# State space decays from turned running sums and two float32r products a step

## The chip, the cores and the metric

One Trainium2 chip, one core. The metric is the device time of one launch in microseconds; the kernel before has a median of 1307.45 us over 3 runs (1307.04 to 1307.95).

## The reference

Two transformer-like blocks on a sequence of 256 rows, width 1024, float32. Only the state space branch of the first block matters here: 32 heads of 64 in 4 groups, state 128, two chunks of 128 positions.

```python
def ssd_chunked(x, dt, a, bm, cm):
    xc = (x * dt[..., None]).reshape(b, c, SSM_CHUNK, g, e, p)
    a_dt = (dt * a).reshape(b, c, SSM_CHUNK, g, e).transpose(0, 1, 3, 4, 2)
    a_cs = jnp.cumsum(a_dt, axis=-1)
    tril = jnp.tril(jnp.ones((SSM_CHUNK, SSM_CHUNK), dtype=bool))
    decay = jnp.exp(jnp.where(tril, a_cs[..., :, None] - a_cs[..., None, :], -jnp.inf))
    cb = jnp.einsum('bclgn,bcsgn->bcgls', cc, bc)
    y_diag = jnp.einsum('bcgls,bcgels,bcsgep->bclgep', cb, decay, xc)
    ...
    y_off = jnp.einsum('bclgn,bcgepn,bcgel->bclgep', cc, prev_states, jnp.exp(a_cs))
    return (y_diag + y_off).reshape(b, l, h, p)
```

For each head and chunk a 128x128 matrix of decays is needed: exp(cs[t] - cs[s]) for s <= t, where cs is the running sum of dt*a, and 0 beyond.

## The kernel before

The program is written out by hand for each engine, in a fixed order, with semaphores between them. Weights come from memory in pieces of 1 MB through four slots (`raw`). ScalarE rounds each piece to float32r (`w_hi`, line 468) and VectorE makes the rest (`w_lo`, line 478, `dve_split`); a large product is three float32r products (lines 529 to 531). A piece may be overwritten only when the piece four before it has been used.

The stage around the change follows the attention branch. TensorE computes `att1`, then `dt`, `bc0`, `bc1` and `xs0` to `xs3` (two pieces each), and turns results back between them. After `dt` VectorE makes dt (lines 1353 to 1358: bias, a minimum, then after ScalarE's exp and log a maximum) and dt*a (line 1361), then splits the two pieces of `bc1`, then convolves `bc0` (line 1394). VectorE's order there is: two merge operations after `att1` (line 1293), a reduction, the split of the second piece of `bc0`, `dve_dt`, the split of both pieces of `bc1`, the convolution of `bc0`, and so on. After `bc1` TensorE makes the running sums with positions down the partitions (`pe_cum`).

Then `pe_ssd` runs 16 steps n, each a group g of 8 heads, a chunk c and a half q of 4 heads, with products of `z0` to `z3` and `gs0` between them as filling:
- GpSimd has made `rows` = upto[s, t] * (dt*a)[s, h], 4 heads of 128 columns (`pool_ssd_rows`, recorded at line 1610), 16 operations of 128x512. The first eight wait only for dt*a, the others for the `ssd_own` that frees their buffer, in two blocks of four.
- `pe_ssd_decay` (line 1627) is one float32 product of `beyond` with these rows, which gives the segment sums in PSUM.
- ScalarE takes exp (line 1634), VectorE multiplies by the masked scores `cb` (line 1643), and TensorE applies the matrix to x*dt (`pe_ssd_own`, line 1654).
- VectorE also has, for each group, the inputs (1559), the state's inputs (1571), skip, late, gate and norm, ScalarE and TensorE the state (1527, 1535, 1549).
GpSimd's remaining work in the stage is four small roots (`pool_z`, line 1852).

The functions that the diff touches, with their callers:

Of the kernel before, what the change touches and what calls it, by code (L numbers as in the profile page):

```python
# [28 lines left out]
NEG = -1.0e30  # L29
# [80 lines left out]
class Kernel:  # L110
# [9 lines left out]
    def memory(self):  # L120
# [33 lines left out]
        half = 4 * KD * SEQ  # L154
        self.stick_l = self.put("stick_l", [P, 2, 2, 384], y_hi_at + half)
        self.stick_w = self.put("stick_w", [P, 2, 2, 384], y_lo_at + half)
        self.rows = self.put("rows", [P, 2, 4, 4, P], y_lo_at)
        self.xc = self.put("xc", [P, 2, MT, GH, SSM_HD], y_hi_at)
        self.xd = self.put("xd", [P, GH, SSM_HD], y_hi_at + 8192)
        self.state = self.put("state", [P, GW], y_hi_at + 12288)  # L160
# [5 lines left out]
        at = self.top = -(-self.top // 128) * 128  # L166
# [67 lines left out]
        self.lat_sq_rows = self.put("mla_squares", [P, MT, 4 * QK + SEQ], y_hi_at + half + 3072)  # L234
        self.rotated = self.put("mla_rotated", [P, MT, 4, 64], y_lo_at + half + 3072)
        self.lat_rows = self.put("mla_latent_rows", [P, MT, Q_RANK + KV_RANK], y_lo_at + half + 5120)
        self.top = at + 42240

    def sb(self, name, shape, dt=F32):
        tensor = self.nc.alloc_sbuf_tensor_at(name, shape, dt, offset=self.top)  # L240
# [108 lines left out]
    def semaphores(self, known):  # L349
        def new(name, unit=1):  # L350
# [30 lines left out]
            new(n) for n in ("dt_act", "dt_dve", "conv_act", "conv_dve", "conv_silu", "xs_turned", "xs_act", "xs_dve"))  # L381
        self.dt_turned = new("dt_turned")
        self.cum_made, self.cum_exp = new("cum_made"), new("cum_exp")
        (self.ssd_rows, self.ssd_cb, self.ssd_bt, self.ssd_bn, self.ssd_xc, self.ssd_xd, self.ssd_cbm, self.ssd_state, self.ssd_state_in,
         self.ssd_off, self.ssd_skip, self.ssd_late, self.ssd_kept, self.ssd_seg, self.ssd_exp, self.ssd_decay, self.ssd_own,
         self.ssd_y) = (new("ssd_" + n) for n in (
             "rows", "cb", "bt", "bn", "xc", "xd", "cbm", "state", "state_in", "off", "skip", "late", "kept", "seg", "exp", "decay",
             "own", "y"))
        self.z_tanh, self.z_read, self.z_gated, self.z_sq, self.z_mean, self.z_root, self.z_norm, self.z_turned, self.z_hi, self.z_lo = (
            new("z_" + n) for n in ("tanh", "read", "gated", "sq", "mean", "root", "norm", "turned", "hi", "lo"))  # L390
# [957 lines left out]
def dve_dt(k):  # L1348
    dve = k.nc.vector
    dt, adt, tmp = (k.dts[:, j, :, :] for j in range(3))  # L1350
    dve.wait_ge(*k.dt_turned.by())
    for m in range(MT):
        t = dve.tensor_tensor(dt[:, m, :], dt_turn_bank(k)[:, SSM_HEADS * m:SSM_HEADS * (m + 1)], k.bcast[:, 0, :], ALU.add)
    t.then_inc(*k.out_dve.at("dt"))
    dve.wait_ge(*k.out_dve.by("dt"))
    dve.tensor_scalar(tmp, dt, 30.0, None, ALU.min).then_inc(*k.dt_dve.at("min"))
    dve.wait_ge(*k.dt_act.by("ln"))
    dve.tensor_tensor(dt, dt, tmp, ALU.max).then_inc(*k.dt_dve.at("dt"))
    dve.wait_ge(*k.dt_dve.by("dt"))
    for m in range(MT):  # L1360
        dve.scalar_tensor_tensor(out=adt[:, m, :], in0=dt[:, m, :], scalar=-1.0, in1=k.bcast[:, 1, :], op0=ALU.mult,
                                 op1=ALU.mult).then_inc(*k.dt_dve.at("adt", m))


def conv_col(k, name, tap, j):
# [60 lines left out]
    dve.tensor_copy(k.y_n[:, 1, c * GW:(c + 1) * GW], k.psum_c[:, 1024 * u + 512:1024 * u + 1024]).then_inc(*k.xs_dve.at(c))  # L1426


def pe_cum(k):
    pe, adt = k.nc.tensor, k.dts[:, 1, :, :]  # L1430
    pe.wait_ge(*k.dt_dve.by("adt", 1))
    for c in range(MT):
        pe.matmul(k.psum_c[:, 32 * c:32 * c + 32], k.upto[:], adt[:, c, :], start=c == 0, stop=True, skip_group_check=True)
    pe.matmul(k.psum_c[:, 64:96], k.beyond[:], adt[:, 0, :], start=False, stop=True, skip_group_check=True).then_inc(*k.cum_made.at())


def act_cum(k):

    act = k.nc.scalar
    act.wait_ge(*k.cum_made.by())  # L1440
    act.activation(k.dts[:, 3, :, :], k.psum_c[:, 0:64].rearrange("p (c h) -> p c h", c=MT), ACT.Copy)
    act.activation(k.dts[:, 4, 0, :], k.psum_c[:, 64:96], ACT.Copy).then_inc(*k.cum_exp.at("copied"))


def act_cum_exp(k):
# [154 lines left out]
    dve.tensor_tensor(x_1, x_1, k.late[:, u, :], ALU.add).then_inc(*k.ssd_kept.at(g))  # L1600


def pool_ssd_rows(k, g):
    pool, u, adt = k.nc.gpsimd, g % 2, k.dts[:, 1, :, :]
    if g >= 2:
        pool.wait_ge(*k.ssd_own.by(g - 2, 1, 1))
    for c in range(MT):
        for q in range(2):
            heads = adt[:, c, g * GH + 4 * q:g * GH + 4 * q + 4].unsqueeze(2).to_broadcast([P, 4, P])
            pool.tensor_tensor(k.rows[:, u, 2 * c + q, :, :], k.upto[:].unsqueeze(1).to_broadcast([P, 4, P]), heads,  # L1610
                               ALU.mult).then_inc(*k.ssd_rows.at(g, c, q))
# [9 lines left out]

def pe_ssd_decay(k, n):
    (g, c, q), pe = ssd_steps()[n], k.nc.tensor
    pe.wait_ge(*k.ssd_rows.by(g, c, q))
    if n >= 2:
        pe.wait_ge(*k.ssd_exp.by(*ssd_steps()[n - 2]))
    pe.matmul(ssd_seg(k, q), k.beyond[:], k.rows[:, g % 2, 2 * c + q, :, :].rearrange("p h t -> p (h t)"), start=True,
              stop=True).then_inc(*k.ssd_seg.at(g, c, q))


def act_ssd_decay(k, n):
    (g, c, q), act = ssd_steps()[n], k.nc.scalar
    act.wait_ge(*k.ssd_seg.by(g, c, q))
    act.activation(k.rows[:, g % 2, 2 * c + q, :, :], ssd_seg(k, q).rearrange("p (h t) -> p h t", h=4),
                   ACT.Exp).then_inc(*k.ssd_exp.at(g, c, q))


def dve_ssd_decay(k, n):
    (g, c, q), dve = ssd_steps()[n], k.nc.vector
    r = k.rows[:, g % 2, 2 * c + q, :, :]  # L1640
    dve.wait_ge(*k.ssd_exp.by(g, c, q))
    dve.wait_ge(*k.ssd_cbm.by(g))
    dve.tensor_tensor(r, r, k.cb[:, g % 2, c, :].unsqueeze(1).to_broadcast([P, 4, P]), ALU.mult).then_inc(*k.ssd_decay.at(g, c, q))


def pe_ssd_own(k, n):
    (g, c, q), pe = ssd_steps()[n], k.nc.tensor
    pe.wait_ge(*k.ssd_decay.by(g, c, q))
    pe.wait_ge(*k.ssd_xc.by(g))
    if g >= 1:  # L1650
        pe.wait_ge(*k.ssd_y.by(g - 1, c))
    for h in range(4):
        at = 512 * c + (4 * q + h) * SSM_HD
        mm = pe.matmul(k.psum_c[:, at:at + SSM_HD], k.rows[:, g % 2, 2 * c + q, h, :], k.xc[:, g % 2, c, 4 * q + h, :],
                       start=q == 0 and h == 0, stop=True, skip_group_check=True)
    mm.then_inc(*k.ssd_own.at(g, c, q))

# [137 lines left out]

# [2003 lines left out]
def tensor_program(k):  # L3799
    pe, A, B = k.nc.tensor, k.psum_a, k.psum_b  # L3800
# [96 lines left out]
def scalar_program(k):  # L3897
# [27 lines left out]
    for u, dst in ((0, k.b_t), (1, k.c_t)):  # L3925
        act_conv_first(k, f"bc{u}", u, 16 + 4 * u)
        act_split(k)
        act_conv_silu(k, f"bc{u}", u, dst)
    act_cum(k)
    for c in range(4):  # L3930
        if c >= 2:
            act.wait_ge(*k.xs_turned.by(c - 2))
        act_conv_first(k, f"xs{c}", c % 2, 4 * c)
        act_split(k)
        act_conv_silu(k, f"xs{c}", c % 2, k.conv[:, c % 2, :, :])
        if c:
            act_turn_back(k, c - 1)
# [83 lines left out]
def vector_program(k):  # L4021
# [175 lines left out]
```

## Time and profile before

| | |
|---|---|
| median of 3 runs | 1307.45 us |
| the profiled execution | 1307.76 us |
| its span, first to last instruction | 1306.2 us |
| TensorE busy | 1286.4 us (98%) |
| VectorE busy | 978.1 us (75%) |
| ScalarE busy | 690.8 us (53%) |
| GpSimd busy | 173.9 us (13%) |
| HBM traffic | 211 MB, 162 GB/s |

The page gives busy time by engine; matmuls are pipelined and their ends modelled, so the distance between starts, or the chain of work that ended last, says more of TensorE than a duration. Durations on VectorE and GpSimd include any time in which the instruction was held after it started. The state space steps run from about 246 to 325 us, the dt and bc work from 159 to 186 us.

### The profile page before, as it was taken

Reading aid. Unit: us, or ns where it says so; the run is one execution under the profiler, and the core shown is the slowest. Engines: PE = TensorE matmul, PEld = TensorE weight load, DVE = VectorE, ACT = ScalarE, POOL = GpSimd, SP = SyncE. Lnnn points to the kernel's source line nnn. Section 1 sums busy time; section 2 is a strip of 40 time slices with the busy share of each in tenths; the row PEclk is TensorE's granted clock in tenths of the full one; section 3 lists DMA queues with packets and bytes.
Section 4 is the critical chain, followed back from the end, with each engine's and each line's share of the span. In section 5 each row is a group of like instructions: output and inputs, shape, how many; then the busy total and the mean of one; then the engine's idle time right before and its main releaser. Section 6 shows DMA issues by size and latency. Waiting matters only on the chain.

```text
span 1306.2 us, 19907 instructions
## 1 busy us (share of the span) xinstructions
PE 1286.4 (98%) x7874; PEld 1118.2 (86%) x7874; DVE 978.1 (75%) x1542; ACT 690.8 (53%) x1014; POOL 173.9 (13%) x241
## 2 busy tenths in 40 slices
PE   8999999999999999999999999999999989999999
PEld 8988999878998998888888877888888867888887
DVE  6457487878646757766667877798888887888888
ACT  5345556535626546633334745655554775655553
POOL 8000030022000000210001231000000160000000
PEclk9999999999999999999999999999999999999999
DMA  9532445522553536476665633266665612376662
GB/s 313 183 128 67 164 165 191 168 91 98 216 188 129 195 129 209 124 206 182 189 201 165 208 129 113 82 208 188 188 190 182 195 60 81 116 207 189 188 203 83
DMA packets 208796, 212.59 MB, mean 163 GB/s; under 512 B 7489, under 2 KB 155923, under 8 KB 208704
## 3 DMA queue, kind: packets, MB, share of 16 engines
q1 hardware_dynamic: 205632, 206.25, 49.7%
q0 software_dynamic: 2480, 4.02, 1.0%
q8 instruction: 63, 1.03, 0.3%
q10 hardware_dynamic: 592, 1.05, 0.2%
q14 instruction: 29, 0.24, 0.1%
HBM read 210.25 MB, written 1.05 MB: 162 GB/s over the span
## 4 chain that ended last, share of the span: by engine, by line
PE 69%; DVE 4%; ACT 3%; issue 2%; POOL 1%; ACTq 0%; DVEq 0%; POOLq 0%
PE psum_b L2206 9%; PE psum_a L2206 9%; PE psum_b L2209 5%; PE psum_a L2209 5%; PE psum_c L529 4%; PE psum_c L530 4%; PE psum_c L531 4%; PE psum_b L529 3%; PE psum_a L529 3%; PE psum_a L531 3%; PE psum_b L531 3%; PE psum_a L530 3%; PE psum_b L530 3%; DVE w_lo L478 1%; PE psum_c L2842 1%
## 5 line engine op out<-in xcount | busy, mean ns | idle before, releaser
L468 ACT ACTIVATE w_hi<-raw 128x2048 fp32r<-128x2048 f32 (+3 forms) x231 | 368.2, 1631 | 24.7 <-PE psum_b L531 12.9
L478 DVE TENSOR_TENSOR w_lo<-raw,w_hi 128x2048 fp32r<-128x2048 f32 (+3 forms) x154 | 342.1, 2237 | 43.8 <-ACT w_hi L468 41.2
L2206 PE MATMUL psum_b<-x,w_hi 128*128 128x512 f32 x528 | 165.6, 395 | 0.0
L2206 PE MATMUL psum_a<-x,w_hi 128*128 128x512 f32 x522 | 164.1, 396 | 0.0
L2209 PEld LDWEIGHTS psum_b<-x,w_lo 128*128 128x128 f32 x528 | 99.2, 188 | 23.2
L491 DVE TENSOR_TENSOR w_lo<-raw,w_hi 128x512 fp32r<-128x512 f32 (+1 forms) x159 | 116.5, 736 | 2.6 <-ACT w_hi L468 2.6
L2209 PEld LDWEIGHTS psum_a<-x,w_lo 128*128 128x128 f32 x522 | 98.0, 188 | 22.8
L2401 POOL CAST ffn_hidden_hi<-ffn_h 128x256 fp32r<-128x256 f32 x66 | 51.0, 773 | 485.3 <-DVE ffn_h L2388 330.3
L2357 ACT ACTIVATE ffn_pre<-ffn_both,cols 128x256 f32<-128x256 f32 x88 | 50.3, 602 | 113.0 <-DVE ffn_both L2369 113.0
L529 PE MATMUL psum_c<-w_hi,ffn_hidden_hi 128*128 128x512 f32 x264 | 103.6, 392 | 0.6 <-DVE ffn_hidden_lo L2393 0.5
L2209 PE MATMUL psum_b<-x,w_lo 128*128 128x256 f32 x528 | 103.7, 278 | 0.0
L530 PE MATMUL psum_c<-w_lo,ffn_hidden_hi 128*128 128x512 f32 x264 | 103.0, 390 | 0.0
L531 PE MATMUL psum_c<-w_hi,ffn_hidden_lo 128*128 128x512 f32 x264 | 102.8, 389 | 0.0
L2209 PE MATMUL psum_a<-x,w_lo 128*128 128x256 f32 x522 | 102.6, 278 | 0.0
L2206 PEld LDWEIGHTS psum_b<-x,w_hi 128*128 128x128 f32 x528 | 82.4, 189 | 2.1
L2206 PEld LDWEIGHTS psum_a<-x,w_hi 128*128 128x128 f32 x522 | 81.7, 189 | 2.3
L2383 DVE SCALAR_TENSOR_TENSOR ffn_pre<-ffn_both,cols,ffn_pre 128x254 f32<-128x254 f32 (+1 forms) x176 | 73.5, 478 | 0.7 <-ACT ffn_pre L2357 0.3
L2369 DVE TENSOR_REDUCE ffn_both<-psum_a 128x256 f32<-128x512 f32 x66 | 42.5, 686 | 37.7 <-PE psum_a L2209 37.7
L2369 DVE TENSOR_REDUCE ffn_both<-psum_b 128x256 f32<-128x512 f32 x66 | 42.5, 686 | 34.6 <-PE psum_b L2209 34.6
L529 PE MATMUL psum_a<-x,w_hi 128*128 128x256 f32 x224 | 64.2, 287 | 1.0 <-DVE x L699 1.0
L529 PE MATMUL psum_b<-x,w_hi 128*128 128x256 f32 x224 | 64.0, 286 | 0.0
L531 PE MATMUL psum_b<-x,w_lo 128*128 128x256 f32 x224 | 63.4, 283 | 0.0
(567 smaller groups left out, 3016.7 us busy)
## 6 DMA issues: line engine op xcount, KB each, us to landing
raw<-in_ffn_w_up_dram SPq DMA_DIRECT2D x88, 512.0 KB, 5.0
raw<-in_w_in_dram SPq DMA_DIRECT2D x39, 1024.0 KB, 5.4
raw<-in_w_gu_dram SPq DMA_DIRECT2D x44, 512.0 KB, 5.0
raw<-in_ffn_w_down_dram SPq DMA_DIRECT2D x44, 512.0 KB, 3.5
raw<-in_w_down_dram SPq DMA_DIRECT2D x22, 512.0 KB, 3.3
raw<-in_w_br_ssm_dram SPq DMA_DIRECT2D x8, 1024.0 KB, 5.0
raw<-in_w_xkv_dram SPq DMA_DIRECT2D x8, 1024.0 KB, 6.3
raw<-in_w_out_dram SPq DMA_DIRECT2D x8, 1024.0 KB, 6.4
```

The lines of the kernel that those rows point to most:

```text
L468: act.activation(k.w_hi[:, s, 0:size], k.raw[:, s, 0:size], ACT.Copy).then_inc(*k.rounded.at(*key))
L478: dve.tensor_tensor(k.w_lo[:, s, 0:size], k.raw[:, s, 0:size], k.w_hi[:, s, 0:size].bitcast(F32), ALU.subtract).then_inc(*k.split.at(*key))
L491: t = dve.tensor_tensor(k.w_lo[:, s, at], k.raw[:, s, at], k.w_hi[:, s, at].bitcast(F32), ALU.subtract)
L529: pe.matmul(out_ap, l[0], r[0], start=start, stop=False, skip_group_check=True)
L530: pe.matmul(out_ap, l[0], r[1], start=False, stop=False, skip_group_check=True)
L531: return pe.matmul(out_ap, l[1], r[0], start=False, stop=stop, skip_group_check=True)
L2206: pe.matmul(ps[:, 512 * j:512 * j + 512].rearrange("p (n t) -> p n t", n=2), hi[j], k.X_both[:, :, kt, :], start=kt == 0, stop=False, skip ...
L2209: mm = pe.matmul(ps[:, 512 * j:512 * j + SEQ], lo[j], k.X[0][:, kt, :], start=False, stop=kt == KD - 1, skip_group_check=True)
L2357: act.activation(k.pre[:, u, j, :], k.both[:, u, j, :], ACT.Identity, scale=ffn_col(k, "ffn_conv_w_2", layer, 2, j, h), bias=ffn_col(k, "f ...
L2369: dve.tensor_reduce(k.both[:, u, j, :], ps[:, 512 * j:512 * j + 512].rearrange("p (n t) -> p t n", n=2), AX, ALU.add).then_inc(*k.ffn_both ...
L2383: dve.scalar_tensor_tensor(out=k.pre[:, u, j, d:], in0=k.both[:, u, j, :SEQ - d], scalar=ffn_col(k, "ffn_conv_w_2", layer, 2 - d, j, h), i ...
L2401: pool.tensor_copy(k.hid[0][:, u, :], k.h32[:, u, :]).then_inc(*k.ffn_hi.at(tag, h))
```

## The change

The decays are made from the running sums themselves. `pe_cum` also makes the sums turned, with the 32 heads down the partitions and the 256 positions along them, from a copy of dt*a in the order half, head, group (`tmp`, two more small VectorE operations in `dve_dt`). They are kept as two float32r parts (`cum_t`; ScalarE the rounded, VectorE the rest). For each of the four (c, q) the ten rows of a product stand at partitions 32n: on one side (`sums_s`) for 4 heads the sums at s in two parts, and two rows of -1; on the other (`sums_t`) the selection of the head in two times four rows, and the sums at t in two parts. One product of these gives cs[s] - cs[t] for 4 heads; a second product ahead of it, `later_r` with the identity, adds 1e30 where s > t; ScalarE's exp has scale -1. GpSimd writes the eight selection rows (4 operations, each 8 partitions by 2048 elements, as soon as `att1` is done) and issues 16 small DMAs from SBUF to SBUF that place the sums. The buffer `rows` holds 4 steps instead of 8, and ScalarE's exp waits for the `ssd_own` four steps before.

```diff
+        self.step_ident = self.put("step_ident", [P, P], masks_at + 4 * 4 * P, F32R)
...
-        self.rows = self.put("rows", [P, 2, 4, 4, P], y_lo_at)
+        self.rows = self.put("rows", [P, 4, 4, P], y_lo_at)
+        self.sums_t = self.put("sums_t", [P, 4, SSM_GROUPS, P], y_lo_at + half, F32R)
+        self.sums_s = self.put("sums_s", [P, SSM_GROUPS, P], y_hi_at + 10240, F32R)
...
@@ dve_dt
+    for m in range(MT):
+        by_step = tmp[:, m, :].rearrange("p (q h g) -> p g q h", q=2, h=4)
+        dve.scalar_tensor_tensor(out=by_step, in0=dt[:, m, :].rearrange("p (g q h) -> p g q h", g=SSM_GROUPS, q=2), scalar=-1.0,
+                                 in1=k.bcast[:, 1, :].rearrange("p (g q h) -> p g q h", g=SSM_GROUPS, q=2), op0=ALU.mult,
+                                 op1=ALU.mult).then_inc(*k.dt_dve.at("adt_turned", m))
@@ pe_cum
-    pe.wait_ge(*k.dt_dve.by("adt", 1))
+    pe.wait_ge(*k.dt_dve.by("adt_turned", 1))
...
+    for c in range(MT):
+        pe.matmul(cum_rows(k)[:, P * c:P * c + P], k.dts[:, 2, c, :], k.upto[:], start=False, stop=True, skip_group_check=True)
...
+def act_cum_rows(k):
+    act = k.nc.scalar
+    act.activation(k.cum_t[0][0:SSM_HEADS, :], cum_rows(k), ACT.Copy).then_inc(*k.cum_act.at("hi"))
+    act.wait_ge(*k.used.by("att1", 1))
+    act.activation(k.sums_s[:, :, :], k.neg_ones[:].unsqueeze(1).to_broadcast([P, SSM_GROUPS, P]), ACT.Copy)
+    act.activation(k.step_ident[:, :], k.ident[:], ACT.Copy)
+    act.activation(k.later_r[:, :], k.strict[:], ACT.Copy, scale=-NEG).then_inc(*k.cum_act.at("ones"))
+
+def dve_cum_rows(k):
+    dve = k.nc.vector
+    dve.wait_ge(*k.cum_act.by("hi"))
+    dve.tensor_tensor(k.cum_t[1][0:SSM_HEADS, :], cum_rows(k), k.cum_t[0][0:SSM_HEADS, :].bitcast(F32),
+                      ALU.subtract).then_inc(*k.cum_dve.at("lo"))
...
-def pool_ssd_rows(k, g):
...
+def step_rows(n, at=0, count=10):
+    return slice(32 * (n % 4) + at, 32 * (n % 4) + at + count)
+
+def pool_ssd_heads(k):
+    pool = k.nc.gpsimd
+    pool.wait_ge(*k.masks.by("ident"))
+    for n in range(4):
+        r, at = step_rows(n, 0, 8), 32 * n
+        first, second = (k.ident[r, at + 4 * j:at + 4 * j + 4].unsqueeze(2).to_broadcast([8, 4, SSM_GROUPS * P]) for j in range(2))
+        pool.tensor_tensor(k.sums_t[r, :, :, :].rearrange("p h g t -> p h (g t)"), first, second, ALU.add).then_inc(*k.sums_made.at("t", n))
+
+def pool_ssd_sums(k):
+    pool = k.nc.gpsimd
+    pool.wait_ge(*k.cum_act.by("ones"))
+    pool.wait_ge(*k.cum_dve.by("lo"))
+    for n in range(4):
+        c, q = n // 2, n % 2
+        for j in range(2):
+            src = k.cum_t[j][16 * q:16 * q + 16, P * c:P * c + P]
+            pool.dma_start(k.sums_t[step_rows(n, 8 + j, 1), :, :, :].rearrange("p h g t -> p (h g) t"), src).then_inc(*k.sums_in.at("t", n, j))
+            pool.dma_start(k.sums_s[step_rows(n, 4 * j, 4), :, :], src).then_inc(*k.sums_in.at("s", n, j))
...
 def pe_ssd_decay(k, n):
     (g, c, q), pe = ssd_steps()[n], k.nc.tensor
-    pe.wait_ge(*k.ssd_rows.by(g, c, q))
+    if n == 0:
+        pe.wait_ge(*k.sums_in.by("s", 3, 1))
+        pe.wait_ge(*k.sums_made.by("t", 3))
     if n >= 2:
         pe.wait_ge(*k.ssd_exp.by(*ssd_steps()[n - 2]))
-    pe.matmul(ssd_seg(k, q), k.beyond[:], k.rows[:, g % 2, 2 * c + q, :, :].rearrange("p h t -> p (h t)"), start=True,
-              stop=True).then_inc(*k.ssd_seg.at(g, c, q))
+    r, seg = step_rows(n), ssd_seg(k, q).rearrange("p (h t) -> p h t", h=4)
+    pe.matmul(seg, k.later_r[:, :], k.step_ident[:, :].unsqueeze(1).to_broadcast([P, 4, P]), start=True, stop=False)
+    pe.matmul(seg, k.sums_s[r, g, :], k.sums_t[r, :, g, :], start=False, stop=True).then_inc(*k.ssd_seg.at(g, c, q))
 
 def act_ssd_decay(k, n):
     (g, c, q), act = ssd_steps()[n], k.nc.scalar
     act.wait_ge(*k.ssd_seg.by(g, c, q))
+    if g:
+        act.wait_ge(*k.ssd_own.by(g - 1, c, q))
...
 def gpsimd_ssd(k):
     k.nc.gpsimd.wait_ge(*k.used.by("att1", 1))
-    k.nc.gpsimd.wait_ge(*k.dt_dve.by("adt", 1))
-    pool_ssd_rows(k, 0)
-    pool_ssd_rows(k, 1)
-    pool_ssd_rows(k, 2)
-    pool_z(k, 0)
-    pool_ssd_rows(k, 3)
-    for g in (1, 2, 3):
+    pool_ssd_heads(k)
+    pool_ssd_sums(k)
+    for g in range(SSM_GROUPS):
         pool_z(k, g)
@@ tensor_program, before the first turn back
             pe.wait_ge(*k.cum_exp.by("copied"))
+            pe.wait_ge(*k.cum_dve.by("lo"))
```

`act_cum_rows` stands behind `act_cum`, `dve_cum_rows` behind the splits that follow the convolution of `bc1`.

## Rows read from the trace of the kernel before

**Rows 1.** The page: busy time of TensorE, and its clock in 40 slices.

```profile
PE 1286.4 (98%) x7874; PEld 1118.2 (86%) x7874; DVE 978.1 (75%) x1542; ACT 690.8 (53%) x1014; POOL 173.9 (13%) x241
...
PEclk9999999999999999999999999999999999999999
```

**Rows 2.** PE's waits, 160 to 340 us (total, times, longest), and line 1627's durations.

```profile
PE psum_a L529 <- DVE gated L1812: 0.5, 1, 0.5
...
L1627 PE MATMUL psum_c<-rows,beyond x32: 590/591/595, 246.6 to 317.7; 128*128 128x512 f32 x32
```

**Rows 3.** The chain that ended last, 285 to 325 us: start, us on the chain, work.

```profile
293.10 0.23 PE psum_a L531
293.33 0.86 PE psum_c L1627 x2
...
300.94 0.50 PE psum_b L1517 x4
...
306.03 1.10 PE psum_b L1527 x2
...
310.20 0.92 PE psum_b L1535 x2
...
322.98 0.84 PE psum_c L1654 x8
```

**Rows 4.** Timeline of POOL and DVE, 167 to 181 us: start, duration, instruction, times.

```profile
168.79 3.08 POOL L1610 TENSOR_TENSOR rows<-upto,dts 128x512 f32<-128x512 f32 x1
176.88 2.03 POOL L1610 TENSOR_TENSOR rows<-upto,dts 128x512 f32<-128x512 f32 x2
167.86 3.12 DVE L478 TENSOR_TENSOR w_lo<-raw,w_hi 128x2048 fp32r<-128x2048 f32 x1 [1.25 <-ACT w_hi L468]
170.90 3.12 DVE L478 TENSOR_TENSOR w_lo<-raw,w_hi 128x2048 fp32r<-128x2048 f32 x1
175.14 5.28 DVE L1394 SCALAR_TENSOR_TENSOR conv<-psum_b,cols,conv 128x255 f32<-128x255 f32 x12 [1.12 <-ACT conv L1375]
```

**Rows 5.** Timeline of DVE, 277 to 321 us.

```profile
277.33 3.12 DVE L478 TENSOR_TENSOR w_lo<-raw,w_hi 128x2048 fp32r<-128x2048 f32 x1
...
319.99 0.69 DVE L1643 TENSOR_TENSOR rows<-rows,cb 128x512 f32<-128x512 f32 x1
```

**Rows 6.** Timeline of DVE and PE, 159 to 174 us, and of ACT at 198.

```profile
159.39 1.29 DVE L1293 TENSOR_TENSOR merged<-psum_b,merged 128x512 f32<-128x512 f32 x2 [1.46 <-PE psum_b L531]
162.75 2.27 DVE L478 TENSOR_TENSOR w_lo<-raw,w_hi 128x2048 fp32r<-128x2048 f32 x1
...
166.31 0.29 DVE L1361 SCALAR_TENSOR_TENSOR dts<-dts,bcast 128x32 f32<-128x32 f32 x2
...
173.76 0.28 PE L531 MATMUL psum_b<-x,w_lo 128*128 128x256 f32 x1
173.88 0.28 PE L529 MATMUL psum_a<-x,w_hi 128*128 128x256 f32 x1
...
197.79 1.93 ACT L1375 ACTIVATE conv<-psum_b,cols 128x256 f32<-128x256 f32 x4 [5.00 <-PE psum_b L531]
```

**Rows 7.** Timeline of POOL and DVE, 27 to 32 us: GpSimd issuing DMAs beside splits.

```profile
29.48 0.61 POOL L1020 DMA_DIRECT2D bcast<-in_dt_bias_dram  x1
...
27.05 4.49 DVE L478 TENSOR_TENSOR w_lo<-raw,w_hi 128x2048 fp32r<-128x2048 f32 x2 [1.74 <-ACT w_hi L468]
```

**Rows 8.** Timeline of POOL and DVE at 762 us: a power beside a split.

```profile
762.23 2.91 POOL L2478 TENSOR_TENSOR fox_rstd<-fox_rstd,half_neg 128x16 f32<-128x16 f32 x1 [22.69 <-DVE fox_rstd L2472]
...
762.26 2.33 DVE L478 TENSOR_TENSOR w_lo<-raw,w_hi 128x2048 fp32r<-128x2048 f32 x1
```

**Rows 9.** Timeline of PE, 3 to 10 us.

```profile
3.02 0.27 PE L1045 MATMUL psum_b<-ident,stage 8*128 8x8 f32 x1 [3.02 <-POOL inv_freq L1004]
3.55 4.21 PE L804 MATMUL psum_a<-ident 128*128 128x128 f32 x18 [0.26 <-DVE cols L1053]
...
8.34 1.73 PE L804 MATMUL psum_a<-ident 128*128 128x128 f32 x14
```

More of the change, by code:

```diff
@@ L132, in memory @@
         self.res = self.sb("res", [P, MT, D])
+        masks_at = self.top
         self.ident, self.ones, self.upto, self.beyond, self.neg_from, self.neg_ones, self.strict, self.causal = (
             self.sb(name, [P, P]) for name in ("ident", "ones", "upto", "beyond", "neg_from", "neg_ones", "strict", "causal"))
+        self.step_ident = self.put("step_ident", [P, P], masks_at + 4 * 4 * P, F32R)
         self.half_neg = self.sb("half_neg", [P, 64])
@@ L156, in memory @@
         self.stick_w = self.put("stick_w", [P, 2, 2, 384], y_lo_at + half)
-        self.rows = self.put("rows", [P, 2, 4, 4, P], y_lo_at)
+        self.rows = self.put("rows", [P, 4, 4, P], y_lo_at)
+        self.sums_t = self.put("sums_t", [P, 4, SSM_GROUPS, P], y_lo_at + half, F32R)
+        self.sums_s = self.put("sums_s", [P, SSM_GROUPS, P], y_hi_at + 10240, F32R)
+        self.cum_t = [self.put(n, [P, SEQ], o, F32R) for n, o in (("cum_t_hi", y_hi_at + 15360), ("cum_t_lo", self.memory_kv_at + 2048))]
         self.xc = self.put("xc", [P, 2, MT, GH, SSM_HD], y_hi_at)
@@ L236, in memory @@
         self.lat_rows = self.put("mla_latent_rows", [P, MT, Q_RANK + KV_RANK], y_lo_at + half + 5120)
-        self.top = at + 42240
+        self.later_r = self.put("later_r", [P, P], at + 42240, F32R)
+        self.top = at + 42752
     def sb(self, name, shape, dt=F32):
@@ L383, in semaphores @@
         self.cum_made, self.cum_exp = new("cum_made"), new("cum_exp")
-        (self.ssd_rows, self.ssd_cb, self.ssd_bt, self.ssd_bn, self.ssd_xc, self.ssd_xd, self.ssd_cbm, self.ssd_state, self.ssd_state_in,
+        self.cum_act, self.cum_dve, self.sums_made, self.sums_in = new("cum_act"), new("cum_dve"), new("sums_made"), new("sums_in", 16)
+        (self.ssd_cb, self.ssd_bt, self.ssd_bn, self.ssd_xc, self.ssd_xd, self.ssd_cbm, self.ssd_state, self.ssd_state_in,
          self.ssd_off, self.ssd_skip, self.ssd_late, self.ssd_kept, self.ssd_seg, self.ssd_exp, self.ssd_decay, self.ssd_own,
          self.ssd_y) = (new("ssd_" + n) for n in (
-             "rows", "cb", "bt", "bn", "xc", "xd", "cbm", "state", "state_in", "off", "skip", "late", "kept", "seg", "exp", "decay",
+             "cb", "bt", "bn", "xc", "xd", "cbm", "state", "state_in", "off", "skip", "late", "kept", "seg", "exp", "decay",
              "own", "y"))
@@ L1426, in dve_turn_back, with cum_rows @@
     dve.tensor_copy(k.y_n[:, 1, c * GW:(c + 1) * GW], k.psum_c[:, 1024 * u + 512:1024 * u + 1024]).then_inc(*k.xs_dve.at(c))
+def cum_rows(k):
+    return k.psum_c[0:SSM_HEADS, P:P + SEQ]
 def pe_cum(k):
     pe, adt = k.nc.tensor, k.dts[:, 1, :, :]
-    pe.wait_ge(*k.dt_dve.by("adt", 1))
+    pe.wait_ge(*k.dt_dve.by("adt_turned", 1))
     for c in range(MT):
         pe.matmul(k.psum_c[:, 32 * c:32 * c + 32], k.upto[:], adt[:, c, :], start=c == 0, stop=True, skip_group_check=True)
+    for c in range(MT):
+        pe.matmul(cum_rows(k)[:, P * c:P * c + P], k.dts[:, 2, c, :], k.upto[:], start=False, stop=True, skip_group_check=True)
     pe.matmul(k.psum_c[:, 64:96], k.beyond[:], adt[:, 0, :], start=False, stop=True, skip_group_check=True).then_inc(*k.cum_made.at())
@@ L1600, in dve_ssd_late @@
     dve.tensor_tensor(x_1, x_1, k.late[:, u, :], ALU.add).then_inc(*k.ssd_kept.at(g))
-def pool_ssd_rows(k, g):
[L1604 to L1611, printed above, removed]
+def step_rows(n, at=0, count=10):
[17 more added lines that the diff above has]
+            pool.dma_start(k.sums_s[step_rows(n, 4 * j, 4), :, :], src).then_inc(*k.sums_in.at("s", n, j))
 def ssd_seg(k, q):
@@ L1633, in act_ssd_decay @@
     act.wait_ge(*k.ssd_seg.by(g, c, q))
-    act.activation(k.rows[:, g % 2, 2 * c + q, :, :], ssd_seg(k, q).rearrange("p (h t) -> p h t", h=4),
-                   ACT.Exp).then_inc(*k.ssd_exp.at(g, c, q))
+    if g:
+        act.wait_ge(*k.ssd_own.by(g - 1, c, q))
+    act.activation(k.rows[:, n % 4, :, :], ssd_seg(k, q).rearrange("p (h t) -> p h t", h=4),
+                   ACT.Exp, scale=-1.0).then_inc(*k.ssd_exp.at(g, c, q))
 def dve_ssd_decay(k, n):
     (g, c, q), dve = ssd_steps()[n], k.nc.vector
-    r = k.rows[:, g % 2, 2 * c + q, :, :]
+    r = k.rows[:, n % 4, :, :]
     dve.wait_ge(*k.ssd_exp.by(g, c, q))
@@ L1653, in pe_ssd_own @@
         at = 512 * c + (4 * q + h) * SSM_HD
-        mm = pe.matmul(k.psum_c[:, at:at + SSM_HD], k.rows[:, g % 2, 2 * c + q, h, :], k.xc[:, g % 2, c, 4 * q + h, :],
+        mm = pe.matmul(k.psum_c[:, at:at + SSM_HD], k.rows[:, n % 4, h, :], k.xc[:, g % 2, c, 4 * q + h, :],
                        start=q == 0 and h == 0, stop=True, skip_group_check=True)
@@ L3929, in scalar_program @@
     act_cum(k)
+    act_cum_rows(k)
     for c in range(4):
@@ L4058, in vector_program @@
         dve_split(k)
+    dve_cum_rows(k)
     for c in range(4):
```

## Prediction

> **What bounds the kernel now.** I read the page first, then the waits of PE between 160 and 340 us, then the chain and the timelines of this stage. TensorE is busy 98% of the span [rows 1]. In the whole stage it waits for another engine once, for 0.5 us [rows 2]. So between 160 and 340 us the time is the sum of PE's work: what PE does less comes off the end, what it waits more is added. The rest of the program hangs on PE's own signals (weight slots come free after their products), so a shift here should reach the end whole.
>
> A decay step today is one float32 product of 128x512, two records, and takes 0.86 us in the chain; a float32r product of the same width takes 0.23 us [rows 3]. There are 16 steps (32 records from 246.6 to 317.7 us) [rows 2].
>
> The second thing to read is GpSimd beside VectorE. One head-row operation of 128x512 takes 1.01 us when nothing is in its way (two in 2.03) [rows 4]. Overlapped with a split of weights, either engine stands still: a split that takes 2.2 us (two in 4.49) [rows 7] took 3.12 us while a GpSimd operation was in flight to 168.79, and the GpSimd operation behind that took 3.08 us, which is the rest of the split plus its own 1.01; the split behind it took 3.12 again although it followed at once [rows 4]. So each VectorE operation with two SBUF inputs waits for the GpSimd operation in flight, to its end, then GpSimd waits for it, in turns. The same at 277 us: again 3.12 for a split [rows 5]. The convolution operations, which read PSUM and one SBUF tile, ran beside GpSimd at their usual 5.28 us for twelve, and GpSimd at its usual 1.01 [rows 4].
>
> **The change, part by part.**
>
> (1) Decay steps. Each float32 product (0.86) becomes two float32r products, the mask product and the ten-row product. No row shows ten rows; bounds are 0.23 each (width decides) and, as the dear end, no gain at all (0.86 for both). I take 0.23, since the width is what the new products share with the row at 0.23. Gain 16 x (0.86 - 0.46) = 6.4 us.
>
> (2) GpSimd's second and third blocks of head rows, at 275 and 297 us, go. In each block the four operations hold three of VectorE's like the split at 277 us (3.12 for 2.25) [rows 5], so VectorE gets back 2.6 us a block. PE gets its own waits back: the 0.5 us [rows 2], which stood behind that late VectorE chain, and 0.18 us at each of two state products (1.10 where 0.92 is usual) [rows 3]. Gain 0.8 us. What is next late: the last decay multiplication on VectorE ends at 320.7, and its products start on PE at 322.98 [rows 3, 5], 2.3 us later. In the VectorE-bound stretch since 297 us PE gains 2.6 us (six steps and one wait) and VectorE 2.6, so that cover stays.
>
> (3) The running sums turned, in pe_cum: two float32 products with a 128-wide moving side, on the chain. The nearest row is 0.50 us for two products of 128x128 [rows 3]. Cost 0.5 us, between 0.2 (32 columns of weights) and 1.0.
>
> (4) ScalarE and VectorE get five operations between bc1 and xs0 (a copy of 32x256, one 128x512, two 128x128; a subtraction of 32x256), some 2 us. Their cover is the wait ahead of every convolution, 5.00 us on ScalarE ahead of xs0's [rows 6], 1.1 on VectorE ahead of bc0's [rows 4]. Cost 0 on the chain; without the cover under 1 us once. The new wait of ScalarE for ssd_own of the group before, and PE's for cum_dve, stand behind products that PE has done by then: 0.
>
> (5) Sixteen GpSimd DMA issues of 0.6 us [rows 7], about 10 us, after the sums, at about 203 us (bc1 from 173.9, 11.5 of products, 1.3 to the convolution, 5.3 and 4.5 for it and two splits, and the stall of part 6). Behind them on GpSimd's queue stand only the four small roots of z, in the steps; the decay products wait for them at 246.6, so there are over 25 us for landing. VectorE's splits ran at 2.25 us beside GpSimd's DMA issues at the start of the kernel [rows 7]. Cost 0.
>
> (6) pool_ssd_heads. This is the part that I price highest. Four operations over 8 partitions, but 2048 elements each along the free side: 4 x 1.01 = 4.0 us each. They wait only for att1, which ended just before VectorE's merge started at 159.39 [rows 6]; the old rows waited for dt*a, made from 166.31 on [rows 6]. So 16 us of GpSimd now lie from 159.4 over the dt chain and the splits of bc0 and bc1. In turns:
> - GpSimd 1: 159.4 to 163.4. The split of the second half of bc0, ready at 162.75, runs 163.4 to 165.6. PE wants it at 168.2 (bc1 starts at 173.88, and half a unit is 48 products of 0.12, the distance of the last two PE rows [rows 6]): no stall.
> - GpSimd 2: 165.6 to 169.6; the minimum over dt (or, if a one-input operation isn't held, the maximum after it) runs at 169.6.
> - GpSimd 3: 169.7 to 173.7; the maximum runs at 173.7.
> - GpSimd 4: 173.85 to 177.9; the four products dt*a (two old, two new, 0.1 each) end at 178.3.
> - Only then, in VectorE's order, the split for bc1: 178.3 to 180.5.
> PE has its last product of bc0 at 173.76 and starts bc1 at 173.88 [rows 6]. It now waits until 180.6: 6.7 us. If the minimum isn't held, the four turns end at the same place, since each of the four GpSimd operations still finds a VectorE operation waiting for it. The second half of bc1 is split by 182.8, when PE wants it at 186: no second stall. VectorE runs the bc0 convolution 183 to 188 and the splits of xs0 to 192.5, when PE comes to it at 192 to 195: just in time.
> The cost of (6) lies between 0 (a long GpSimd operation over 8 partitions doesn't hold VectorE: one of 2.91 us, a power, left a split beside it at 2.33 [rows 8]) and 6.7. I take 6.7, because the only streaming additions and products that the trace has beside VectorE held it to their end each time [rows 4, 5], and the power reads 16 elements and then computes.
> What the Trainium skill says of it (GPSIMD Engine Reference, Key points): GpSimd shares its SBUF interfaces with VectorE, which collide where a VectorE instruction has two SBUF inputs or a 2-port mode. The trace agrees, with 0.84 us for each held operation. Its section Performance versus the Vector engine gives 4497 ns for a float32 tensor_tensor of 2048 elements; with that the stall would be some 2 us longer than the sum has it.
>
> (7) A PE that stood for 6.7 us may come back slow. The page's clock row reads full all through [rows 1], but pitch tells: after its 3.0 us without work at the start of the kernel, PE needed 4.21 us for 18 products of 128x128 (0.23 each), and from 8.3 us on 1.73 for 14 (0.12 each) [rows 9], half rate, that is 1.2 instead of 2.4 GHz, for some 4.5 us. At half rate that loses 2.3 us. Bounds 0 and 3.4. I take 2.3, because 6.7 is more standing still than the 3.0 of that row.
> The Trainium skill (TensorE: Matmul & The Clock Gate, Part 1) has an idle engine fall to 1.2 GHz and come back under load; by that rule the 2.3 us are due, without it the sum ends at no change.
>
> **Sum.** -6.4 - 0.8 + 0.5 + 6.7 + 2.3 = +2.3 us. The profiled execution has 1307.76 us, span 1306.2 and 1.6 around it, 0.3 above the median 1307.45. The forecast is 1307.45 + 2.3 = 1309.8.
>
> **Rivals.**
> - *No hold.* The heads' operations don't hold VectorE, or only for short pieces, and (6) and (7) vanish: -6.4 - 0.8 + 0.5 = -6.7, 1300.8. For it: the power row; 8 of 128 partitions. Against: every streaming operation in rows 4 and 5. With a hold of half the length the turns end at 170 to 171, the split at 173, and PE hardly waits: also about 1301. In between (holds of 3 us) 1302 to 1306.
> - *Slower: heads dearer than 4.0 us.* If one takes 4.5 us (more than four times the short one, or both inputs broadcast), the four turns end 2 us later and PE stalls 8.7: +4.3, 1311.8. It decides from 4.1 us per operation on, where the total passes the 0.2% line.
> - *Stall, but PE returns at full clock:* +0.0, 1307.5.
> - *The change doesn't do what it says:* the ten-row or the broadcast product costs as much as the old one; then the 6.4 isn't there and even the stall-free case ends at 1307, with the stall at 1316. For it only that no row shows such a product.
>
> **How the numbers follow.** Forecast 0.40 (1308.5 to 1311), dearer heads 0.17, full clock 0.11, no or short hold 0.27, no gain in the decay steps 0.05. A measurement can tell about 0.2%, 2.6 us, from no change, so "same" is 1304.8 to 1310.1. Faster: the no-hold case and its in-between, 0.30. Slower: the upper part of the forecast, dearer heads and most of no gain, 0.34. Same: 0.36. Eight in ten need both ends: 1300.8 to 1312.6. The likeliest case's own range is 1308.5 to 1311.
>
> **What would show it.** Right: PE idle of 5 to 9 us at 174, released by a split; GpSimd's four operations from 159.4, some of them 6 us long with VectorE's turns in them; VectorE's dt operations of 2 to 4 us; products at double pitch behind the stall; the decay step at 0.46 in the chain; no GpSimd beside VectorE at 275. Wrong: no idle at 174 with the heads at 4 us each beside undisturbed splits (then 1300.8), or a decay step that is not 0.46. I would be wrong as well if a new wait shows at 246 to 256 (DMAs late) or at 322.

## The result and the profile after

The changed kernel takes 1314.12 us (median of 4 runs, 1312.65 to 1314.66) against 1307.59 us of the kernel before beside it (median of 4). The ratio is 1.0047, 95% interval 1.0035 to 1.0059: slower, by some 6 us or 0.5%, and above the upper end of the range, 1312.6. The profiled execution has a span of 1312.3 us, 6.1 more than before's 1306.2. Line numbers of the changed kernel are higher: 478 has become 485, 529 to 531 have become 536 to 538.

First the page of the changed kernel: the totals, and the clock in 40 slices, to be read beside [rows 1].

```profile
PE 1288.8 (98%) x7878; PEld 1119.6 (85%) x7878; DVE 981.4 (75%) x1545; ACT 692.2 (53%) x1018; POOL 171.7 (13%) x245
...
PEclk9999989999999999999999999999999999999999
```

The one digit 8 is the slice from 164 to 197 us. PE's waits between 160 and 340 us (total, times, longest) have one entry, where [rows 2] had the 0.5 us:

```profile
PE psum_a L536 <- DVE w_lo L485: 4.8, 1, 4.8
```

The busy time in three stretches there (PE, PEld, DVE, ACT, POOL, then the granted clock, the DMA share and GB/s):

```profile
160.00:170.00 10.00, 10.00 (x80) 9.19 (x78) 7.90 (x7) 3.96 (x6) 9.84 (x3) 1.00 0.53 186
170.00:180.00 10.00, 5.21 (x38) 5.03 (x37) 9.96 (x7) 9.59 (x9) 5.81 (x2) 0.80 0.05 7
180.00:190.00 10.00, 10.00 (x74) 10.00 (x74) 9.86 (x15) 1.26 (x2) 0.00 (x0) 0.85 0.63 216
```

The timeline of GpSimd and VectorE in that stretch, after:

```profile
159.35 16.54 POOL L1650 TENSOR_TENSOR sums_t<-ident 8x2048 fp32r<-8x2048 f32 x4 [126.58 <-PE psum_b L538]
162.49 2.59 DVE L485 TENSOR_TENSOR w_lo<-raw,w_hi 128x2048 fp32r<-128x2048 f32 x1
165.01 0.27 DVE L1360 TENSOR_TENSOR dts<-psum_c,bcast 128x32 f32<-128x32 f32 x2
165.32 3.28 DVE L1363 TENSOR_SCALAR dts<-dts 128x64 f32<-128x64 f32 x1
169.21 3.08 DVE L1365 TENSOR_TENSOR dts<-dts 128x64 f32<-128x64 f32 x1 [0.61 <-ACT dts L1346]
172.33 3.70 DVE L1368 SCALAR_TENSOR_TENSOR dts<-dts,bcast 128x32 f32<-128x32 f32 x2
175.96 0.31 DVE L1372 SCALAR_TENSOR_TENSOR dts<-dts,bcast 128x32 f32<-128x32 f32 x2
176.16 4.48 DVE L485 TENSOR_TENSOR w_lo<-raw,w_hi 128x2048 fp32r<-128x2048 f32 x2
```

These are the turns: one VectorE operation per GpSimd operation, each held for what is left of it. Operations of 0.2 us (unheld, the minimum takes 0.20 and the maximum 0.22, as the first experiment shows, and the first two products of dt*a 0.29 [rows 6]) take 3.3, 3.1 and 3.7 us, and the one-input minimum (TENSOR_SCALAR) is held like the others; the two that read PSUM (line 1360, 0.27) pass at once. The split that bc1 waits for starts at 176.16, in VectorE's order behind all of it. PE's restart, from its timeline:

```profile
178.59 0.55 PE L536 MATMUL psum_a<-x,w_hi 128*128 128x256 f32 x1 [4.79 <-DVE w_lo L485]
178.94 0.41 PE L537 MATMUL psum_a<-x,w_hi 128*128 128x256 f32 x1
179.15 0.41 PE L538 MATMUL psum_a<-x,w_lo 128*128 128x256 f32 x1
...
183.08 0.28 PE L536 MATMUL psum_a<-x,w_hi 128*128 128x256 f32 x1
183.19 0.28 PE L537 MATMUL psum_a<-x,w_hi 128*128 128x256 f32 x1
```

Starts lie 0.21 us apart to 182.8 and 0.12 from 183 on: about 4.3 us at the slower pace after 4.8 us of standing still. The granted clock of the same trace is 0.50 (1.2 GHz) from 178.6 to 182.8 us and 1.00 (2.4 GHz) from 184 us on.

The surprise is in the steps. The chain of the changed kernel (start, us on the chain, work), to be read beside [rows 3]:

```profile
263.32 0.23 PE psum_a L538
263.55 0.23 PE psum_c L1682
263.78 0.43 PE psum_c L1683
264.21 0.43 PE psum_a L536
```

The mask product (1682) takes the 0.23 us of its width, the ten-row product (1683) 0.43, and the ordinary product behind it 0.43 too. The two new products and what they add behind them are 0.23 + 0.43 + 0.20 = 0.86 us, what the one float32 product cost, whose follower took the usual 0.23 us.

### The profile page after: what moved, and what is told of

The parts are those of the page before. It is cut to its first block, busy times and chain, and to the rows that moved or that the text cites. A ratio compares the mean times of both kernels' runs of the same rounds, so it can differ in the third digit from the quotient of the medians.

```text
span 1312.3 us, 19926 instructions
## 1 busy us (share of the span) xinstructions
PE 1288.8 (98%) x7878; PEld 1119.6 (85%) x7878; DVE 981.4 (75%) x1545; ACT 692.2 (53%) x1018; POOL 171.7 (13%) x245
## 4 chain that ended last, share of the span: by engine, by line
PE 88%; DVE 5%; ACT 4%; issue 2%; POOL 1%; ACTq 0%; POOLq 0%; DVEq 0%
PE psum_b L2259 9%; PE psum_a L2259 9%; PE psum_a L536 6%; PE psum_a L538 6%; PE psum_a L537 6%; PE psum_b L536 6%; PE psum_b L538 5%; PE psum_b L537 5%; PE psum_c L536 5%; PE psum_b L2262 5%; PE psum_a L2262 5%; PE psum_c L537 5%; PE psum_c L538 5%; DVE w_lo L485 2%; PE psum_c L1711 1%
## 5 line engine op out<-in xcount | busy, mean ns | idle before, releaser
L2262 PE MATMUL psum_b<-x,w_lo 128*128 128x256 f32 x528 | 103.7, 278 | 0.0
L2262 PE MATMUL psum_a<-x,w_lo 128*128 128x256 f32 x522 | 102.6, 278 | 0.0
L536 PE MATMUL psum_a<-x,w_hi 128*128 128x256 f32 x224 | 65.2, 291 | 5.3 <-DVE w_lo L485 4.8
L537 PE MATMUL psum_a<-x,w_hi 128*128 128x256 f32 x224 | 64.2, 287 | 0.0
L538 PE MATMUL psum_a<-x,w_lo 128*128 128x256 f32 x224 | 64.1, 286 | 0.0
```

Source lines behind the costliest of these rows:

```text
L536: pe.matmul(out_ap, l[0], r[0], start=start, stop=False, skip_group_check=True)
L537: pe.matmul(out_ap, l[0], r[1], start=False, stop=False, skip_group_check=True)
L538: return pe.matmul(out_ap, l[1], r[0], start=False, stop=stop, skip_group_check=True)
L2262: mm = pe.matmul(ps[:, 512 * j:512 * j + SEQ], lo[j], k.X[0][:, kt, :], start=False, stop=kt == KD - 1, skip_group_check=True)
```

## The books of the difference

Starts of the same work in the two traces give where the time went. The work of `bc1` starts at 178.59 instead of 173.88: +4.7. It ends, where `pe_cum` begins, at 192.07 instead of 185.41: +6.7, so 2.0 in bc1's half-rate stretch. `xs0` starts at 193.32 instead of 185.99: +7.3, so 0.7 for `pe_cum` with its two added products. The second of the four turns of z starts at 339.56 instead of 333.36: +6.2, so 1.1 are gained over all 16 steps, of which 0.8 are PE's small waits of [rows 2, 3]. From there to the end nothing changes: +6.1.

## Experiments

The first question is whether GpSimd's head operations cause the stall, and in which way; the second why the steps gained nothing.

### The heads beside the convolutions

```diff
     for n in range(4):
         r, at = step_rows(n, 0, 8), 32 * n
+        pool.wait_ge(*k.conv_act.by(("bc0", "bc1", "xs0", "xs1")[n], 0))
```

> Each of GpSimd's four head operations waits for the first convolution signal of bc0, bc1, xs0 and xs1 in turn, so that it runs beside VectorE operations that read PSUM; nothing else is changed. Theory (VectorE is held by the head operations, PE stalls 4.8 us at 174 and runs 1.9 us longer over bc1 at half rate): stall and slow stretch vanish, VectorE's dt operations return to 0.2 to 0.3 us, 1314.1 - 6.7 = 1307.4 us. Rival (the stall comes from the longer dt chain itself or from the new order): the stall stays, 1313 to 1314 us.

Measured: 1306.48 us against 1307.11 (0.9997, interval 0.9987 to 1.0006), 7.6 under the changed kernel's 1314.1, 1 us better than expected. The two were measured in different series; taken against the kernel before beside each, the step is from +6.5 to -0.6, 7.2 us. In the trace 0.3 us of the gain lie ahead of this stage, where the merge starts at 158.88 instead of 159.14. VectorE and GpSimd:

```profile
164.74 0.20 DVE L1363 TENSOR_SCALAR dts<-dts 128x64 f32<-128x64 f32 x1
165.54 0.22 DVE L1365 TENSOR_TENSOR dts<-dts 128x64 f32<-128x64 f32 x1 [0.61 <-ACT dts L1346]
...
174.63 5.27 DVE L1406 SCALAR_TENSOR_TENSOR conv<-psum_b,cols,conv 128x255 f32<-128x255 f32 x12 [2.79 <-ACT conv L1387]
...
174.77 3.59 POOL L1651 TENSOR_TENSOR sums_t<-ident 8x2048 fp32r<-8x2048 f32 x1 [142.04 <-ACT conv L1387]
```

PE no longer waits at 174, and its clock stays at 1.00. The twelve convolution operations take 5.27 us with GpSimd's 3.59 inside them: neither holds the other. So the same four operations do no harm at another place. The row also gives the price of one undisturbed, 3.59 us, where I had 4.0.

### The heads in 16 short operations at the old place

```diff
-        pool.tensor_tensor(k.sums_t[r, :, :, :].rearrange("p h g t -> p h (g t)"), first, second, ALU.add).then_inc(*k.sums_made.at("t", n))
+        for h in range(4):
+            o = pool.tensor_tensor(k.sums_t[r, h, :, :].rearrange("p g t -> p (g t)"), first[:, h, :], second[:, h, :], ALU.add)
+        o.then_inc(*k.sums_made.at("t", n))
```

> GpSimd's four head operations of 2048 elements are cut into 16 of 512, at the same place; nothing else is changed. Theory (VectorE is held to the end of the one operation in flight): GpSimd's total stays 16 us, but each VectorE operation is held under 1 us, so the split for bc1 comes at 175 to 176 instead of 178.6, PE stalls 1 to 2.5 us and keeps its full rate: 1308 to 1310 us. Rival (VectorE gets no turn while GpSimd has work queued): 1314 us as before.

Measured: 1306.28 us (0.9995, 0.9986 to 1.0005), better than my 1308 to 1310: PE doesn't stall at all. VectorE, and GpSimd's row:

```profile
165.04 0.72 DVE L1363 TENSOR_SCALAR dts<-dts 128x64 f32<-128x64 f32 x1
166.37 0.52 DVE L1365 TENSOR_TENSOR dts<-dts 128x64 f32<-128x64 f32 x1 [0.61 <-ACT dts L1346]
166.93 1.03 DVE L1368 SCALAR_TENSOR_TENSOR dts<-dts,bcast 128x32 f32<-128x32 f32 x2
167.88 1.16 DVE L1372 SCALAR_TENSOR_TENSOR dts<-dts,bcast 128x32 f32<-128x32 f32 x2
168.94 6.17 DVE L485 TENSOR_TENSOR w_lo<-raw,w_hi 128x2048 fp32r<-128x2048 f32 x2
...
159.39 24.77 POOL L1651 TENSOR_TENSOR sums_t<-ident 8x512 fp32r<-8x512 f32 x16 [125.45 <-PE psum_b L538]
```

The operations are held as before, but for 0.3 to 0.9 us each, so the two splits are done at 175.1 instead of 180.6, and the first of them, the one that PE waits for, is done before PE needs it. GpSimd's work lasts longer (24.8 us with its own waits, against 16.5) and costs nothing. So it is the length of one operation that VectorE pays for, not GpSimd's total.

### Three heads at the old place

```diff
         r, at = step_rows(n, 0, 8), 32 * n
+        if n == 3:
+            pool.wait_ge(*k.conv_act.by("bc0", 0))
```

> The changed kernel with the fourth of GpSimd's head operations moved beside the convolution of bc0, the first three where they are. Theory (turns of one held VectorE operation per GpSimd operation of 3.6 us): the last turn ends near 172.3, the split for bc1 near 175.1, PE stalls 1.3 to 1.5 us instead of 4.8. If a short stall keeps the full rate, 1314.1 - 3.4 - 1.9 = 1308.8 us; if any stall costs the 1.9 us at half rate, 1310.7 us.

Measured: 1307.84 us (1.0011, 1.0002 to 1.0020), 1 us under the 1308.8 and far from the 1310.7 (the kernel before beside it, 1306.70, is 0.9 below the one beside the changed kernel). PE waits 1.4 us for the split, as expected, and goes on at full rate. Its waits and the chain behind them:

```profile
PE psum_a L536 <- DVE w_lo L485: 1.4, 1, 1.4
...
172.90 2.19 DVE w_lo L485
175.09 0.14 issue
175.22 0.36 PE psum_a L536
...
176.17 0.12 PE psum_a L536
176.29 0.12 PE psum_a L537
```

The starts are 0.12 us apart at once, and the granted clock stays at 1.00. So the 2 us at half rate belong to the longer stall.

### The second product over 128 rows, and over 10

The plain form, the two tiles of the changed kernel read over all 128 rows, gave no time, neither alone nor with the heads moved: the other rows hold leftovers. The ten rows must be alone in a product of full height. So ScalarE writes the selection rows for all four (c, q) in one operation of 128x2048 (1.90 us, before bc1's convolution, where it waited anyway) with zeros elsewhere, from columns that VectorE makes earlier in three small operations, and the weights' side stands four times, once for each (c, q), zero outside its ten rows. That takes 8 KB a partition, for which the buffer of x is used; x is loaded again with the memory rows. GpSimd only issues DMAs. The core of it:

```diff
+def act_heads(k):
+    act = k.nc.scalar
+    act.wait_ge(*k.used.by("att1", 1))
+    act.wait_ge(*k.sums_made.by("sel"))
+    act.activation(k.sums_t[:, :, :, :].rearrange("p h g t -> p h (g t)"), k.sel_s[:, 0:4].unsqueeze(2).to_broadcast([P, 4, SSM_GROUPS * P]),
+                   ACT.Copy).then_inc(*k.cum_act.at("heads"))
...
-    r, seg = step_rows(n), ssd_seg(k, q).rearrange("p (h t) -> p h t", h=4)
+    r, seg = slice(0, P), ssd_seg(k, q).rearrange("p (h t) -> p h t", h=4)
...
-    pe.matmul(seg, k.sums_s[r, g, :], k.sums_t[r, :, g, :], start=False, stop=True).then_inc(*k.ssd_seg.at(g, c, q))
+    pe.matmul(seg, k.sums_s[r, n % 4, g, :], k.sums_t[r, :, g, :], start=False, stop=True).then_inc(*k.ssd_seg.at(g, c, q))
```

> ScalarE writes the selection rows in one operation over 128 partitions (the other rows become 0) and GpSimd makes none; the weights' side stands four times, once a step, with 0 outside the step's ten rows, in the buffer of x, which is loaded again later; and each step's second product goes over all 128 rows. Theory (few rows keep the weights from loading ahead): the second product costs 0.23 us and so does the one behind it, a step falls from 0.86 to 0.46 us, 16 x 0.40 = 6.4 us under the version with the heads beside the convolutions (1306.5): 1300.1 us. Rival (the strided moving side or the second product of a bank costs): a step stays at 0.86 us and the time at 1306.5 us.

> The same kernel as f1_rows_128 but for one slice: the second product of a step goes over its ten rows. Theory: 0.2 us before and 0.2 us after it again, a step at 0.86 us, 1306.5 us; the pair with f1_rows_128 then is worth 6.4 us. Rival: the same time as f1_rows_128.

The second differs from the first by one line:

```diff
-    r, seg = slice(0, P), ssd_seg(k, q).rearrange("p (h t) -> p h t", h=4)
+    r, seg = step_rows(n), ssd_seg(k, q).rearrange("p (h t) -> p h t", h=4)
```

Measured, on one chip: 1300.33 us over 128 rows (0.9946, interval 0.9931 to 0.9961) and 1307.18 over ten (1.0003, 0.9993 to 1.0013). The spans are 1298.5 and 1305.2: 6.7 us for the number of rows, of which the steps are 6.4 (16 times 0.40 in the chain). With both effects gone the changed kernel is 7.0 us under the kernel before; parts 1 to 3 of the prediction, without stall and half rate, come to 6.7. The rival of the expectation is out too: the second product keeps its strided moving side and its place in the bank, and costs 0.23 us. The chains, first over 128 rows, then over ten:

```profile
301.26 0.23 PE psum_c L1697
301.50 0.24 PE psum_c L1698
301.74 0.23 PE psum_a L537
```

```profile
301.90 0.23 PE psum_c L1697
302.13 0.42 PE psum_c L1698
302.55 0.43 PE psum_a L537
```

Where the 0.2 us come from is in the timeline of the weight loads, first the changed kernel's, then the 128-row one's:

```profile
253.65 0.19 PEld L1682 LDWEIGHTS psum_c<-step_ident,later_r 128*128 128x128 f32 x1
254.19 0.18 PEld L1683 LDWEIGHTS psum_c<-sums_t,sums_s 10*128 10x128 f32 x1 [0.35 <-issue]
254.62 0.19 PEld L1682 LDWEIGHTS psum_c<-step_ident,later_r 128*128 128x128 f32 x1 [0.25 <-issue]
255.05 0.18 PEld L1683 LDWEIGHTS psum_c<-sums_t,sums_s 10*128 10x128 f32 x1 [0.24 <-issue]
255.47 0.19 PEld L536 LDWEIGHTS psum_a<-w_hi,x 128*128 128x128 f32 x1 [0.25 <-issue]
```

```profile
246.45 0.19 PEld L1697 LDWEIGHTS psum_c<-step_ident,later_r 128*128 128x128 f32 x1
246.67 0.19 PEld L1698 LDWEIGHTS psum_c<-sums_t,sums_s 128*128 128x128 f32 x1
246.90 0.19 PEld L1697 LDWEIGHTS psum_c<-step_ident,later_r 128*128 128x128 f32 x1
```

At equal heights loads follow one another every 0.23 us, each beside the product ahead of it. Around a ten-row product they are 0.42 to 0.54 us apart and the loader stands 0.24 to 0.35 us: neither the ten rows' weights nor those behind load beside the other product, though the load itself takes the same 0.18 us. The Trainium skill (TensorE: Matmul & The Clock Gate, Part 2) has weights pulled ahead when row groups don't conflict or when they go to the background buffer. This case agrees with it between products of 128 rows; between ten and 128 the weights were not pulled ahead.

The trace of the kernel before has such a change of height too, in the attention of the second block, where eight products of 64 rows, eight of 32 and two of 128 follow one another:

```profile
1060.77 0.52 PEld L3495 LDWEIGHTS psum_c<-mla_rope_t 32*128 32x128 f32 x8 [0.33 <-issue]
1061.62 0.30 PEld L3498 LDWEIGHTS psum_c<-causal_r,ident_r 128*128 128x128 f32 x2 [0.33 <-issue]
```

The loader stands 0.33 us ahead of the first load of each new height and not between the eight of one height. These eight go to the two halves of the rows in turn, so it stays open whether short products over the same rows, one behind another, would load ahead.

### Ten rows at partition 0, and 64 rows

```diff
-    r, seg = step_rows(n), ssd_seg(k, q).rearrange("p (h t) -> p h t", h=4)
+    r, seg = step_rows(0), ssd_seg(k, q).rearrange("p (h t) -> p h t", h=4)
```

> As f2_rows_10, with the ten rows of partitions 0 to 9 in all 16 steps (all steps take the rows of steps 0, 4, 8 and 12, so the decays are not the reference's). If the narrowness costs, a step stays at 0.86 us (0.23 for the mask product, 0.43 for the ten rows, 0.2 on the product behind). If it is the start at partition 32, 64 or 96 that costs, all steps fall to 0.46 us; the four steps with rows at 0 in f2_rows_10 would be short too.

```diff
-    r, seg = step_rows(n), ssd_seg(k, q).rearrange("p (h t) -> p h t", h=4)
+    r, seg = slice(64 * (n % 4 // 2), 64 * (n % 4 // 2) + 64), ssd_seg(k, q).rearrange("p (h t) -> p h t", h=4)
```

> As f1_rows_128, with the second product over the 64 rows (0 to 63 or 64 to 127) that hold the step's ten. Theory (anything under the full height): a step at 0.86 us. Rival (only a product of one row group of 32): 0.46 us.

One run each: 1307.05 us with ten rows at 0 (whose decays are not the reference's) and 1306.44 with 64 rows, beside 1307.3 of the kernel before. The step is read from the chains, which don't hang on the spread of single runs. In both it stays as over ten rows; with 64 rows the chain reads

```profile
301.66 0.23 PE psum_c L1697
301.89 0.42 PE psum_c L1698
302.31 0.43 PE psum_a L537
```

So the start partition has no part in it, and half the height is as dear as ten rows.

### The heads put back on the best kernel

```diff
+    for n in range(4):
+        r, at = step_rows(n, 0, 8), 32 * n
+        first, second = (k.ident[r, at + 4 * j:at + 4 * j + 4].unsqueeze(2).to_broadcast([8, 4, SSM_GROUPS * P]) for j in range(2))
+        pool.tensor_tensor(k.sums_t[r, :, :, :].rearrange("p h g t -> p h (g t)"), first, second, ALU.add).then_inc(*k.heads_made.at("t", n))
```

> f1_rows_128 with GpSimd's four head operations put back at their place in the changed kernel (ScalarE's operation, later, writes the same rows again and waits for them). Theory: the stall and the half rate alone, 4.8 + 1.9 = 6.7 us on top of 1300.3: 1307.0 us. Rival (with the shorter decay steps part of the stall is made up, or VectorE becomes the bound behind it): 1304 to 1306 or 1308 and more.

Measured: 1307.54 us (1.0007, 0.9997 to 1.0016, single runs from 1305.85 to 1309.25), 7.2 over the 1300.33 where 6.7 were expected; against the kernel before beside each it is 7.8. PE waits 4.7 us in it, for nothing else in the stage, and the clock of 170 to 190 us reads as in the changed kernel:

```profile
170.00:180.00 10.00, 5.27 (x39) 5.09 (x38) 9.96 (x7) 9.37 (x9) 5.58 (x2) 0.82 0.06 9
180.00:190.00 10.00, 10.00 (x73) 10.00 (x73) 9.86 (x15) 3.07 (x3) 0.00 (x0) 0.84 0.63 217
```

The two effects, stall and rows, are of about one size and add up to within about 1 us: without both the kernel is 7.0 us under the kernel before beside it, with one of them between 0.8 under and 0.8 over, with both 6.5 over. The 1 us is not resolved, since these times come from different series.

## Why the prediction was wrong

The mechanism that was forecast to eat the gain is there, but the gain was not. The step that failed is the first term of the sum, 6.4 us for the decay steps. Step by step:

- **Part 1, the decay steps, failed.** I put each of the two products at the 0.23 us of its width and took 6.4 us; measured 0. I had named the bound (0.86 for both) and given it 0.05, with 1316 us as the time that it makes with the stall; the time came out at 1314.1. The wrong choice was to take the price of a product from the width alone. The row at 0.23 is that of a product among neighbours of the same shape. What the new product has not in common with them is its height: ten rows cost 0.43 us and 0.20 more on the product behind, the same product over 128 rows 0.23 and nothing. The trace of before had the nearer rows, the two weight loads at 1060.77 and 1061.62 us with 0.33 us of standing ahead of each; I did not look for their price.
- **Part 2, PE's small waits, right:** 0.8 of the 1.1 us that the steps gave back. These waits are gone and nothing late took their place, nor does anything in the kernel at 1300.3, where PE waits for no engine from 150 to 340 us.
- **Part 3, pe_cum:** 0.7 against 0.5.
- **Parts 4 and 5 right:** the added ScalarE and VectorE operations and the 16 DMA issues, from 203.92 to 212.7 us, cost nothing.
- **Part 6, the stall, right in kind, too large:** 4.8 against 6.7 us. The turns came in the order given; the one-input minimum was held, too. A head operation takes 3.59 us, not 4.0, which over four is 1.6 of the 1.9 us that the stall was shorter. With the 0.3 of part 7 this hid about 2 us of the miss of 6.4 in part 1; that the sum missed by only some 4 us is luck to that extent.
- **Part 7, half rate:** 2.0 against 2.3 us, and only behind the 4.8 us stall: one of 1.4 us left the rate alone.

With the measured terms the sum is 0 - 0.8 + 0.7 + 4.8 + 2.0 = +6.7 us, against +6.1 in the span and +6.5 in the medians. The rest (0.3 in the steps beside the waits, and 0.25 us by which the program was already earlier at 159 us, as its merge starts at 159.14 instead of 159.39) is not explained further.

Of the rivals, "no hold" and "full clock" are out by the timeline. "Dearer heads" would have given 1311.8 by a longer stall, which did not happen. The measured case is "the change doesn't do what it says", with 0.05 the least likely of the five, for the ten-row product and not for the broadcast one.

## What to carry to other kernels

In these traces GpSimd additions and products of 512 or 2048 elements a partition held each VectorE operation with two SBUF inputs, and the one-input minimum from SBUF to SBUF, until they ended; VectorE operations that read PSUM ran beside them. Keep such operations short where VectorE feeds a chain, or lay them beside VectorE work that reads PSUM. And a small product among full-height ones can be worth padding with zero rows to their height: here it brought 0.40 us for each product and cost no time, but 8 KB a partition and a second load of x. When a new product is priced, its neighbours belong to the price.

## What the runs showed of the hardware that was not expected

- A float32r product of 10 or of 64 rows (512 wide) between products of 128 rows costs 0.43 us instead of 0.23, and so does the one behind it; ten rows at partition 0 in every step cost the same as at 0, 32, 64 and 96.
- A one-input float32 operation on VectorE of 128x64, SBUF to SBUF, was held 3.1 us (3.28 instead of 0.20) by GpSimd like a two-input one.
- A GpSimd addition of 8x2048 with both inputs broadcast takes 3.59 us, less than four products of 128x512 at 1.01.
- After 4.8 us without work PE went on at a granted clock of 0.50 for about 4.3 us, after 1.4 us at 1.00.
